# Adding the expert rows in DRAM with an accumulating scatter, instead of storing two rows per token and summing them on TensorE

## The chip, the cores and the metric

The kernel runs on one core of one Trainium2 chip. The metric is the device time of one execution in microseconds (us). Before the change the median of three runs was 1459.46 us (1457.72 to 1459.51).

## The reference

One encoder layer is applied to two sequences, 512 and 1024 tokens of 1024 numbers (T = 1536 tokens in all, 12 tiles of 128). What matters for the change is its last part, the mixture of experts and the norm behind it. Every token chooses one group and in it two of the 32 experts; the outputs of the two are weighted and added.

```python
def block_fn(args):
    tok, w, e = args
    xb = h_pad[tok]
    gu = xb @ w_gate_up[e]
    y = (jax.nn.silu(gu[:, :D_EXPERT]) * gu[:, D_EXPERT:]) @ w_down[e]
    return y * w[:, None]
yb = lax.map(block_fn, (buf_tok..., buf_w..., block_e))
out = jnp.zeros((t_tok + 1, d), h.dtype).at[buf_tok].add(yb.reshape(rows, d))
...
x = layer_norm(ALPHA * x + g2 * moe(h), ln2_g, ln2_b)
```

## The kernel before, in words

There is no scheduler: every engine has its own instruction stream, written out by hand, and the engines meet at semaphores. The stages follow each other.

**Adaptation and input projection.** w_ada comes in 24 pieces of 1 MB (`load_ada`). The first 12 are used ahead of everything else. The other 12 are spread over the first six token tiles of the input projection (`ADA_TILES` = 6, the loop at L427 of the SP queue): each piece goes through one SBUF slot, is split by ScalarE (`ada_h`, L693) and VectorE (`ada_l`, L944), and is multiplied on TensorE (`ada_mm`, L1342 and L1343). The token tiles themselves come through one buffer, `xs` (`load_x`, L399). All these loads leave by one queue, SP's, and each waits until its buffer is free.

**Mixing, second norm, routing.** These write h2 (the experts' input) and x1 (the residual) to DRAM and make a table of the blocks: which 128 token rows each block gathers, where it scatters them, with which weights, and which expert it belongs to. There are 39 blocks here for 32 experts. An unused row of a block has an index that is out of bounds, and its row is not written.

**Expert blocks.** For block i, POOL gathers the rows (`gather`, L645), TensorE transposes them and computes gate and up, then down for block i-1; each product is three matmuls of 512 columns (L1320, L1321, L1322), since the numbers are held as a high and a low part. ScalarE splits the weights (L815, L819), VectorE takes the remainders (L1220, L1224). SP loads 6 MB of weights for each new expert, each piece as soon as its slot is free (L487, L495). ScalarE weighs the result into the one buffer `y_sb` (`weigh`, L846), and POOL scatters it into DRAM (`scatter`, L656). `scatter(i)` waits for the landing of the scatter before it, then copies its indices `s_idx` (L651) and its weights `s_w` (L652), on which `weigh` waits, and then issues the transfer. A pair (token, choice) has a row of its own: `y_rows` has 3072 rows, choice 0 in the first 1536, choice 1 behind them.

**Final stage.** The SP queue loads the second norm's vectors and all 12 tiles of x1 into `fin` (L541) while the last blocks run, waits for all scatters, and loads for each token tile the two rows of each token (`y0`, L547, and `y1`, L548; four slots). TensorE adds them: two products with the identity for each half of 512 columns, four matmuls for a tile, into two banks (L1619, L1620). VectorE multiplies the banks with the gate (`gated`, L1280, 128x512 twice), adds the residual (L1284), and does the norm in a pipeline over the tiles: variance of tile t-1 (L1290), gain of tile t-1 (L1294), scale and shift of tile t-2 (L1299). ScalarE squares (L895) and stores the tiles, POOL takes the power -0.5 (L675).

## Time and profile before

| | |
|---|---|
| median of three runs | 1459.46 us (1457.72 to 1459.51) |
| time of the profiled execution | 1457.56 us |
| its span | 1455.8 us |
| mean granted TensorE clock | 0.94 |
| TensorE matmul | 1266.5 us busy, 87% of the span |
| TensorE weight load | 1030.7 us, 71% |
| VectorE | 932.9 us, 64% |
| ScalarE | 653.3 us, 45% |
| GpSimd (POOL) | 280.3 us, 19% |
| read from and written to DRAM | 297.47 MB and 39.37 MB |

The first 657 us hold projection, mixing and routing, the stretch from 657 to 1370 us the expert blocks, and the last 85 us the final stage. A share is an average over these stages, so what bounds each stage is read from a stretch of it. "SPq" is an instruction on the SP queue that issues a transfer; "[4.88 <-DMA ada_raw]" at the end of a timeline row says that the engine stood idle for 4.88 us before it and what ended that.

### The profile page before, as it was taken

To read this page: it belongs to the slowest core of one execution; us is meant where nothing else is said; L and a number is where in the kernel's file an instruction comes from. 1 tells how busy PE (TensorE), PEld (TensorE's weight loads), DVE (VectorE), ACT (ScalarE), POOL (GpSimd) and SP (SyncE) were. 2 spreads that over 40 slices of the span, in tenths; PEclk is the share of its full clock that TensorE was granted. 3 is DMA by queue.
4 is the path that set the end of the run, shared out by engine and by line. 5 is a ranking of instruction groups with operands and counts; after the bars stand their busy time and mean duration, and the time that the engine had idled before them with its cause. 6 is when DMAs were issued, how large, how long until landed. Compare 5 with 4: busy or idle time off the path is not lost.

```text
span 1455.8 us, 22916 instructions
## 1 busy us (share of the span) xinstructions
PE 1266.5 (87%) x6239; PEld 1030.7 (71%) x6240; DVE 932.9 (64%) x1025; ACT 653.3 (45%) x635; POOL 280.3 (19%) x321
## 2 busy tenths in 40 slices
PE   4479999999789799426999999999999999999592
PEld 3367888788668588325888888888888888888440
DVE  7655544443356455595657875765478888888188
ACT  5532322111212112215556765665478888887222
POOL 6100000000024344241111211111112111222122
PEclk9889999999989899558999999999999999999896
DMA  9642231000233432634769996877689999998793
GB/s 296 246 143 93 96 102 57 18 29 1 92 125 116 144 115 101 243 132 168 263 245 344 402 366 226 307 261 269 226 342 396 398 397 395 388 406 310 307 348 138
DMA packets 111712, 329.44 MB, mean 226 GB/s; under 512 B 12192, under 2 KB 37952, under 8 KB 111680
## 3 DMA queue, kind: packets, MB, share of 16 engines
q1 hardware_dynamic: 98288, 288.63, 53.4%
q0 software_dynamic: 11520, 34.09, 6.3%
q10 hardware_dynamic: 1872, 6.29, 1.1%
q8 instruction: 20, 0.33, 0.1%
q14 instruction: 12, 0.10, 0.0%
HBM read 297.47 MB, written 39.37 MB: 231 GB/s over the span
## 4 chain that ended last, share of the span: by engine, by line
PE 77%; DVE 14%; DMA 3%; issue 2%; ACT 2%; POOL 1%; SPq 1%; DVEq 0%; POOLq 0%; ACTq 0%
PE bank L1320 21%; PE bank L1322 21%; PE bank L1321 21%; PE bank L1552 2%; PE bank L1342 1%; PE bank L1343 1%; PE bank L1516 1%; PE bank L1574 1%; DVE ada_l L944 1%; DVE hT L968 1%; DVE fin L1284 1%; DVE fin L1299 1%; DVE gated L1280 1%; PE bank L1407 1%; ACT ada_h L693 1%
## 5 line engine op out<-in xcount | busy, mean ns | idle before, releaser
L1220 DVE TENSOR_TENSOR gu_l<-gu_raw,gu_h x124 | 278.5, 2287 | 39.7 <-ACT gu_h L815 39.7
L1320 PE MATMUL bank<-gu_h,xT_h 128*128 (+1 forms) x624 | 248.1, 398 | 4.1 <-DVE xT_l L1239 4.1
L1322 PE MATMUL bank<-gu_h,xT_l 128*128 (+1 forms) x624 | 244.5, 392 | 0.0
L1321 PE MATMUL bank<-gu_l,xT_h 128*128 (+1 forms) x624 | 243.9, 391 | 0.0
L815 ACT ACTIVATE gu_h<-gu_raw (+1 forms) x128 | 238.4, 1924 | 5.2 <-issue 5.2
L1224 DVE TENSOR_TENSOR dn_l<-dn_raw,dn_h (+1 forms) x64 | 143.6, 2285 | 5.9 <-ACT dn_h L819 5.9
L1320 PEld LDWEIGHTS bank<-gu_h,xT_h 128*128 128x128 f32 x624 | 117.8, 189 | 28.1 <-DVE xT_l L1239 2.9
L1320 PE MATMUL bank<-win_h,hT_h 128*128 128x512 f32 x288 | 117.4, 408 | 22.5 <-DMA pool_s<-in_pool_scale 22.5
L1322 PEld LDWEIGHTS bank<-gu_h,xT_l 128*128 128x128 f32 x624 | 117.7, 189 | 25.5
L1321 PEld LDWEIGHTS bank<-gu_l,xT_h 128*128 128x128 f32 x624 | 118.0, 189 | 23.7
L819 ACT ACTIVATE dn_h<-dn_raw (+1 forms) x64 | 119.0, 1914 | 33.9 <-DVE table_i L1215 33.8
L1320 PE MATMUL bank<-dn_h,aT_h 128*128 (+1 forms) x312 | 125.6, 402 | 2.5 <-DVE aT_l L1234 2.5
L1322 PE MATMUL bank<-dn_h,aT_l 128*128 (+1 forms) x312 | 122.5, 393 | 0.0
L1321 PE MATMUL bank<-dn_l,aT_h 128*128 (+1 forms) x312 | 122.4, 392 | 0.0
L1322 PE MATMUL bank<-win_h,hT_l 128*128 128x512 f32 x288 | 114.4, 397 | 0.0
L1321 PE MATMUL bank<-win_l,hT_h 128*128 128x512 f32 x288 | 114.4, 397 | 0.0
L656 POOL DMA_INDIRECT y_rows<-y_sb,s_idx x39 | 66.7, 1710 | 221.1 <-ACT y_sb L846 221.1
L825 ACT ACTIVATE act_s<-bank 128x512 f32<-128x512 f32 x39 | 23.3, 597 | 183.4 <-PE bank L1322 183.4
L1320 PE MATMUL bank<-wout_h,z_h 128*128 128x512 f32 x192 | 79.1, 412 | 14.3 <-DVE z_l L1063 14.3
L944 DVE TENSOR_TENSOR ada_l<-ada_raw,ada_h 128x2048 fp32r<-128x2048 f32 x24 | 55.2, 2307 | 45.0 <-ACT ada_h L693 44.8
L1230 DVE TENSOR_TENSOR act_a<-bank,act_s 128x512 f32<-128x512 f32 x39 | 27.0, 691 | 85.7 <-ACT act_s L825 85.7
L1320 PEld LDWEIGHTS bank<-win_h,hT_h 128*128 128x128 f32 x288 | 55.1, 191 | 34.3 <-DMA pool_s<-in_pool_scale 22.8
(226 smaller groups left out, 2144.5 us busy)
## 6 DMA issues: line engine op xcount, KB each, us to landing
gu_raw<-in_w_gate_up SPq DMA_DIRECT2D x128, 1024.0 KB, 7.5
dn_raw<-in_w_down SPq DMA_DIRECT2D x64, 1024.0 KB, 7.5
ada_raw<-in_w_ada SPq DMA_DIRECT2D x24, 1024.0 KB, 5.5
y<-y_rows SPq DMA_DIRECT2D x24, 512.0 KB, 5.4
win_raw<-in_w_in SPq DMA_DIRECT2D x8, 768.0 KB, 6.9
h_rows<-h SPq DMA_DIRECT2D x12, 512.0 KB, 2.7
x_rows<-x SPq DMA_DIRECT2D x12, 512.0 KB, 3.6
fin<-x_rows SPq DMA_DIRECT2D x12, 512.0 KB, 13.7
```

What stands on the lines that cost most here:

```text
L656: nc.gpsimd.indirect_dma_start(out=y_d, out_offset=bass.IndirectOffsetOnAxis(ap=s_idx[:, 0:1], axis=0), in_=y_sb[:], in_offset=None, bound ...
L815: nc.scalar.activation(gu_slot(gu_h, e, c), gu_slot(gu_raw, e, c), ACT.Copy).then_inc(S["gu_split_h"], 1)
L819: nc.scalar.activation(dn_slot(dn_h, e, c), dn_slot(dn_raw, e, c), ACT.Copy).then_inc(S["dn_split_h"], 1)
L825: nc.scalar.activation(act_s[:], ps[0][:], ACT.Silu).then_inc(S["silu_made"], 1)
L944: nv.tensor_tensor(ada_l[slot][:], ada_raw[slot][:], ada_h[slot][:].bitcast(F32), ALU.subtract).then_inc(S["ada_split_l"], 1)
L1220: nv.tensor_tensor(gu_slot(gu_l, e, c), gu_slot(gu_raw, e, c), gu_slot(gu_h, e, c).bitcast(F32), ALU.subtract).then_inc(S["gu_split_l"], 1)
L1224: nv.tensor_tensor(dn_slot(dn_l, e, c), dn_slot(dn_raw, e, c), dn_slot(dn_h, e, c).bitcast(F32), ALU.subtract).then_inc(S["dn_split_l"], 1)
L1230: nv.tensor_tensor(act_a[:], ps[1][:], act_s[:], ALU.mult).then_inc(S["act_ready"], 1)
L1320: mm(out, lh, rh, start=start, stop=False)
L1321: mm(out, lh, rl, start=False, stop=False)
L1322: return mm(out, ll, rh, start=False, stop=stop)
L1552: last = nc.tensor.transpose(ps[2 + k // 4][:, (k % 4) * P:(k % 4 + 1) * P], xg[:, k * P:(k + 1) * P], ident[:])
```

## The change

1. `y_rows` has 1536 rows, one per token, and both choices of a token have the same row index (the iota at L620 has step 0 between them in place of T).
2. The indirect transfer of `scatter` gets `compute_op=ALU.add`: it adds the block's rows to what is in DRAM. Blocks stay apart, since each waits for the one before it to land, and one block holds a token once.
3. The rows must be zero first. POOL clears a tile `zeros` (128x128) at its very start, and SP writes it into `y_rows` with 12 transfers of 512 KB, two in front of each turn of the `ADA_TILES` loop. Each transfer reads the 512 B of a partition eight times. POOL waits for them before the first gather.
4. The final stage loads one tile of rows per token tile in place of two, TensorE has no part in it, and VectorE multiplies `y0` in SBUF with the gate in one instruction of 128x1024. The slot of `y0` is free once `gated` is made.

```diff
-        TOP0 = top // 32 * 32 - 3744
+        TOP0 = top // 32 * 32 - 3744 - 4 * ZN
...
-        y_d = nc.dram_tensor("y_rows", (PAIRS, D), F32).ap()
+        y_d = nc.dram_tensor("y_rows", (T, D), F32).ap()
...
             load_ada(N_ADA1)
             load_x(1, 0)
+            sp.wait_ge(S["zeros_made"], 1)
             for t in range(ADA_TILES):
+                for n in range(t * NT // ADA_TILES, (t + 1) * NT // ADA_TILES):
+                    sp.dma_start(y_d[n * P:(n + 1) * P, :].rearrange("p (c n) -> p c n", n=ZN), zeros[:, None, :].to_broadcast([P, D // ZN, ZN])).then_inc(S["y_zeroed"], 16)
                 load_x(t + 2, 0 if t + 2 < SEQ_TILES[0][1] else 1)
                 load_ada(N_ADA1 + 2 * t + 1)
...
                 if t >= F_SLOTS:
-                    sp.wait_ge(S["y_summed"], t - F_SLOTS + 1)
+                    sp.wait_ge(S["f_gated"], t - F_SLOTS + 1)
                 sp.dma_start(y0[s][:], y_d[bass.ds(t * P, P), :]).then_inc(y_loaded[s], 16)
-                sp.dma_start(y1[s][:], y_d[bass.ds(T + t * P, P), :]).then_inc(y_loaded[s], 16)
...
+            pool.memset(zeros[:], 0.0).then_inc(S["zeros_made"], 1)
             st.done(pool.memset(ident[:], 0.0))
...
-            nc.gpsimd.iota(tok[:], pattern=[[T, 2], [P, NT]], base=0, channel_multiplier=1,
+            nc.gpsimd.iota(tok[:], pattern=[[0, 2], [P, NT]], base=0, channel_multiplier=1,
...
-                                             in_=y_sb[:], in_offset=None, bounds_check=PAIRS - 1,
-                                             oob_is_err=False).then_inc(S["y_scattered"], 16)
-
+                                             in_=y_sb[:], in_offset=None, bounds_check=T - 1,
+                                             oob_is_err=False, compute_op=ALU.add).then_inc(S["y_scattered"], 16)
+
+            pool.wait_ge(S["y_zeroed"], 16 * NT)
             gather(0, first=True)
...
-                dve.wait_ge(S["y_summed"], t + 1)
-                for b in range(2):
-                    c = slice(512 * b, 512 * (b + 1))
-                    last = nv.tensor_tensor(gated[:, c], ps[bank + b][:], g2b[q][:, c], ALU.mult)
+                dve.wait_ge(y_loaded[t % F_SLOTS], 16 * (t // F_SLOTS + 1))
+                if t >= 1:
+                    dve.wait_ge(S["f_taken"], t)
+                last = nv.tensor_tensor(gated[:], y0[t % F_SLOTS][:], g2b[q][:], ALU.mult)
                 last.then_inc(S["f_gated"], 1)
...
-            for t in range(NT):
-                slot, bank = t % F_SLOTS, 2 * (t % F_BANKS)
-                pe.wait_ge(y_loaded[slot], 32 * (t // F_SLOTS + 1))
-                if t >= F_BANKS:
-                    pe.wait_ge(S["f_gated"], t - F_BANKS + 1)
-                for b in range(2):
-                    n = slice(512 * b, 512 * (b + 1))
-                    mm(ps[bank + b][:], ident[:], y0[slot][:, n], start=True, stop=False)
-                    last = mm(ps[bank + b][:], ident[:], y1[slot][:, n], start=False, stop=True)
-                last.then_inc(S["y_summed"], 1)
```

The SP queue at the start of the `ADA_TILES` loop (`ada_raw` is a piece of w_ada, `xs` a token tile), before:

```order
L399 DMA xs<-in_x_prompt 128x1024 [waits xT_made] x2
L394 DMA ada_raw_69<-in_w_ada 128x8x256 [waits ada_used] x2
L399 DMA xs<-in_x_prompt 128x1024 [waits xT_made]
L394 DMA ada_raw_69<-in_w_ada 128x8x256 [waits ada_used] x2
L399 DMA xs<-in_x_sample 128x1024 [waits xT_made]
```

and after:

```order
L400 DMA xs<-in_x_prompt 128x1024 [waits xT_made]
L432 DMA y_rows<-zeros 1024x1x128 [waits zeros_made]
L432 DMA y_rows<-zeros 1024x1x128
L400 DMA xs<-in_x_prompt 128x1024 [waits xT_made]
L395 DMA ada_raw_69<-in_w_ada 128x8x256 [waits ada_used] x2
L432 DMA y_rows<-zeros 1024x1x128 x2
L400 DMA xs<-in_x_prompt 128x1024 [waits xT_made]
L395 DMA ada_raw_69<-in_w_ada 128x8x256 [waits ada_used] x2
L432 DMA y_rows<-zeros 1024x1x128 x2
L400 DMA xs<-in_x_sample 128x1024 [waits xT_made]
```

In the first turn the two writes stand behind a token tile; in the other five they stand right behind the second of two pieces of w_ada and ahead of the next token tile.

VectorE at the start of the final stage, before:

```order
L1280 TENSOR_TENSOR gated<-bank,g2b_218 128x512 [waits y_summed,last_loaded]
L1280 TENSOR_TENSOR gated<-bank,g2b_218 128x512
L1284 SCALAR_TENSOR_TENSOR fin_204,f_sum<-fin_204,gated 128x1024 [waits x1_loaded0,f_gated]
L1286 TENSOR_SCALAR f_mean<-f_sum 128x1 [waits f_taken]
L1280 TENSOR_TENSOR gated<-bank,g2b_218 128x512 [waits y_summed]
```

and after:

```order
L1285 TENSOR_TENSOR gated<-y_0_197,g2b_215 128x1024 [waits y_loaded0,last_loaded]
L1289 SCALAR_TENSOR_TENSOR fin_201,f_sum<-fin_201,gated 128x1024 [waits x1_loaded0,f_gated]
L1291 TENSOR_SCALAR f_mean<-f_sum 128x1 [waits f_taken]
L1285 TENSOR_TENSOR gated<-y_1_198,g2b_215 128x1024 [waits f_taken,y_loaded1]
L1289 SCALAR_TENSOR_TENSOR fin_202,f_sum<-fin_202,gated 128x1024 [waits x1_loaded0,f_gated]
```

Two instructions on banks have become one on a loaded tile, and what it waits for is the load itself.

## Rows read from the trace of the kernel before

**Rows 1.** The page's chain that ended last: shares of the span.
```profile
PE 77%; DVE 14%; DMA 3%; issue 2%; ACT 2%; POOL 1%; SPq 1%; DVEq 0%; POOLq 0%; ACTq 0%
```
**Rows 2.** Timeline from last block to second tile: start us, us, engine, line, operation, [idle].
```profile
1368.32 0.18 POOL L651 COPY s_idx<-table_i 128x1 int32 x1 [6.50 <-DMA y_rows<-y_sb,s_idx]
1368.44 0.18 POOL L652 COPY s_w<-table 128x1 f32 x1
1368.98 1.26 ACT L846 ACTIVATE y_sb<-bank,s_w 128x512 f32<-128x512 f32 x2 [8.58 <-PE bank L1322]
1371.13 0.99 POOL L656 DMA_INDIRECT y_rows<-y_sb,s_idx  x1 [2.51 <-ACT y_sb L846]
1378.36 0.33 SPq L547 DMA_DIRECT2D y<-y_rows  x1
...
1383.27 2.07 PE L1619 MATMUL bank<-y,ident 128*128 128x512 f32 x2 [14.40 <-DMA y<-y_rows]
...
1388.85 1.29 DVE L1280 TENSOR_TENSOR gated<-bank,g2b 128x512 f32<-128x512 f32 x2 [27.40 <-PE bank L1620]
...
1390.17 1.23 DVE L1284 SCALAR_TENSOR_TENSOR fin<-fin,gated 128x1024 f32<-128x1024 f32 x1
...
1392.21 1.29 DVE L1280 TENSOR_TENSOR gated<-bank,g2b 128x512 f32<-128x512 f32 x2 [0.62 <-PE bank L1620]
```
**Rows 3.** Groups of VectorE by form: xcount, busy us, mean ns of one, idle before.
```profile
L1280 DVE TENSOR_TENSOR gated<-bank,g2b 128x512 f32<-128x512 f32 x24 | 15.4, 683 | 28.0 <-PE bank L1620 28.0
...
L962 DVE TENSOR_TENSOR hT_l<-hT,hT_h 128x1024 fp32r<-128x1024 f32 x12 | 14.6, 1218 | 0.0
```
**Rows 4.** Windows, us: PE, PEld, DVE, ACT, POOL busy, clock, DMA share, GB/s.
```profile
1062.56:1328.36 265.80, 265.80 (x1261) 220.97 (x1261) 237.82 (x151) 211.87 (x181) 54.49 (x75) 1.00 1.01 394
1368.00:1377.00 9.00, 0.86 (x4) 0.38 (x2) 0.00 (x0) 1.26 (x2) 1.30 (x3) 0.79 1.03 413
```
**Rows 5.** DMA view, 1060 to 1350 us: queue's packets, MB; issues, us to landing.
```profile
q0 software_dynamic: 4752, 12.55, 11.3%
...
gu_raw<-in_w_gate_up SPq DMA_DIRECT2D x61, 1024.0 KB, 7.6
...
y_rows<-y_sb,s_idx POOLq DMA_INDIRECT x17, 8.3
```
**Rows 6.** DMA view, 1360 to 1379 us, two scatters: POOL's queue.
```profile
q0 software_dynamic: 396, 1.02, 13.5%
```
**Rows 7.** Timeline of one expert block, 1148 to 1168 us.
```profile
1149.00 2.15 POOL L656 DMA_INDIRECT y_rows<-y_sb,s_idx  x1 [6.05 <-ACT y_sb L846]
1149.69 8.55 SPq L487 DMA_DIRECT2D gu_raw<-in_w_gate_up  x4
...
1159.15 1.91 ACT L815 ACTIVATE gu_h<-gu_raw  x1
...
1164.56 1.27 ACT L846 ACTIVATE y_sb<-bank,s_w 128x512 f32<-128x512 f32 x2
```
**Rows 8.** Timeline, 2 to 9 us: a transfer with later ones queued behind it.
```profile
2.40 0.58 SPq L402 DMA_DIRECT2D w_spT<-in_w_spatial  x1
3.02 8.25 SPq L394 DMA_DIRECT2D ada_raw<-in_w_ada  x4
...
8.07 1.12 PE L1332 MATMUL bank<-ident,w_spT 128*128 128x128 f32 x4 [4.32 <-DMA w_spT<-in_w_spatial]
```
**Rows 9.** Timeline of one piece of w_ada, and the window while it moves.
```profile
103.85 0.38 SPq L394 DMA_DIRECT2D ada_raw<-in_w_ada  x1
...
109.12 1.91 ACT L693 ACTIVATE ada_h<-ada_raw 128x2048 fp32r<-128x2048 f32 x1 [4.88 <-DMA ada_raw<-in_w_ada]
```
```profile
106.00:107.00 1.00, 1.00 (x6) 0.83 (x5) 0.00 (x0) 0.00 (x0) 0.00 (x0) 1.00 1.06 371
```
**Rows 10.** Timeline, 0 to 2 us: POOL's clear and VectorE's first work.
```profile
0.77 0.20 POOL L553 MEMSET ident<- 128x128 f32 x1 [0.29 <-POOLq L1635]
...
1.79 0.23 DVE L921 TENSOR_SCALAR bands<-band_prev 128x128 f32<-128x128 f32 x1 [1.67 <-POOL band_prev L559]
```

More of the change, by code:

```diff
@@ L53 @@
 F_SLOTS = 4
+ZN = 128
 F_BANKS = 4
@@ L170, in encoder @@
         half_neg = r.take("half_neg", [P, 1])
+        zeros = r.take("zeros", [P, ZN])
         r = Region(C1)
@@ L288, in encoder @@
         y0 = [r.take(f"y0_{s}", [P, D]) for s in range(F_SLOTS)]
-        y1 = [r.take(f"y1_{s}", [P, D]) for s in range(F_SLOTS)]
         fin = [r.take(f"fin{t}", [P, D]) for t in range(NT)]
@@ L329, in encoder @@
         S = {n: sem(n) for n in (
-            "c_loaded small_loaded ada_bias c_silu cT_made biasT_made cT_high cT_low bias_copied pair_sum_made ada_split_h ada_split_l mod_hl_made mod_cols mod_made modT_made ident_made"
+            "zeros_made y_zeroed c_loaded small_loaded ada_bias c_silu cT_made biasT_made cT_high cT_low bias_copied pair_sum_made ada_split_h ada_split_l mod_hl_made mod_cols mod_made modT_made ident_made"
             " consts_made mod_row mod_stored wsp_loaded wspT_made wspT_copied band_edge"
@@ L348, in encoder @@
             " y_idx y_scattered"
-            " last_loaded y_summed f_gated f_taken f_centre f_squared f_var f_rstd_made f_gained f_ready f_stored"
+            " last_loaded f_gated f_taken f_centre f_squared f_var f_rstd_made f_gained f_ready f_stored"
             " dve_steps pool_steps dve_carrier pool_carrier sp_carrier"
@@ L1275, in f_residual @@
             def f_residual(t):
-                q, bank = 0 if t < SEQ_TILES[0][1] else 1, 2 * (t % F_BANKS)
-                dve.wait_ge(S["y_summed"], t + 1)
-                for b in range(2):
-                    c = slice(512 * b, 512 * (b + 1))
-                    last = nv.tensor_tensor(gated[:, c], ps[bank + b][:], g2b[q][:, c], ALU.mult)
+                q = 0 if t < SEQ_TILES[0][1] else 1
+                dve.wait_ge(y_loaded[t % F_SLOTS], 16 * (t // F_SLOTS + 1))
+                if t >= 1:
+                    dve.wait_ge(S["f_taken"], t)
+                last = nv.tensor_tensor(gated[:], y0[t % F_SLOTS][:], g2b[q][:], ALU.mult)
                 last.then_inc(S["f_gated"], 1)
```

## The prediction

> **What bounds the kernel now.** I began with the chain that ended last [rows 1]: TensorE carries 77% of the span and VectorE 14%, so removing TensorE work pays only where TensorE is the last to finish. The matmuls that go are in the final stage, so I read its timeline [rows 2]. The last scatter is issued at 1371.13, the first load of y leaves at 1378.36 when it has landed, TensorE begins at 1383.27 and VectorE at 1388.85. From there VectorE sets the end: of the 28.0 us that it stands idle ahead of its 24 instructions on `gated` [rows 3], 27.40 are ahead of tile 0 and 0.62 ahead of tile 1, so later tiles wait for nothing. So the sum is on the path only at the stage's start. Then the windows of the expert blocks [rows 4]: from 1062.56 to 1328.36, which I chose as 15 blocks of 17.72 us with a new expert each, TensorE is busy for all of it, and the DMA engines show a share of 1.01 at 394 GB/s. That is the second thing to see. TensorE bounds the blocks, but the transfers are nearly full as well, and the change alters a transfer there. Last, the early loads [rows 8, 9], beside which the zeros are written.
>
> **The final stage.** In 1378.36 to 1388.85 there are two parts. TensorE's first sum takes 1388.85 - 1383.27 = 5.58 us and goes. The load before it takes 4.91 us for two transfers of 0.52 MB; with one to wait for, 0.52 MB less at the 413 GB/s of a full queue [rows 4] is 1.27 us less, 3.64 us. So VectorE starts 10.49 - 3.64 = **6.85 us** earlier after the scatter's landing. This holds if transfers of one queue finish in the order of issue; rows 8 bear that out (below). Tile 1 needs the second load, 4.91 us after 1378.36, and VectorE is done with tile 0 at 3.64 + 2.7: its wait of **0.62 us** goes and no other takes its place. The instruction on `gated` changes: the two halves on banks took 1390.17 - 1388.85 = 1.32 us to the start of the next, and the nearest row of one 128x1024 instruction with both inputs in SBUF is `hT_l` with 1.218 us [rows 3], with the 0.03 us to the next 1.25. That is 0.07 us x 12 tiles = **0.8 us**; if it takes as long as the pair it is 0. The added wait on `f_taken` costs nothing, since the instruction ahead of it in VectorE's own queue has waited for the same count. Loads of tiles 4 to 11 now wait for `gated` of three tiles before, some 14 us ahead of their use (three tiles of four instructions of about 1.2 us) against a landing of 4 to 5 us. Together -8.3 us.
>
> **The scatter.** No row shows an accumulating transfer. I call x what it takes longer to land than a plain one. It is paid twice at the end. `s_idx` of the last block waits for the scatter before it until 1368.32, `s_w` is done at 1368.62, and `weigh` starts at 1368.98 because of TensorE: 0.36 us of cover, then every microsecond is on the path. The last scatter pays x again before the loads of y. So 2x - 0.36 us. The bound below is x = 0: the same bytes are written. For the value: an addition in DRAM must read the 0.51 MB that it writes. The two last scatters moved 1.02 MB [rows 6], and the queue is full with the x1 tiles until 1377, at 413 GB/s; 0.51 MB more is 1.24 us. I take x = 1.3. The bound above is that the transfer takes as long again as the whole landing, 7.2 us (1371.13 to 1378.36). I stay near the lower end because most of the 7.2 us is not bytes of the scatter (0.51 MB is 1.24 us of it) but issue, the other queue's packets and completion, which an addition does not repeat. **+2.2 us**.
>
> The Trainium skill ("Collectives: The Full Stack", the bandwidth ceiling) has a rule that speaks against this change: the adding unit itself costs nothing, but the addition needs two source reads on the same read ring, which halved the measured rate of a reduction against a copy (1.93 times). By it each scatter's data phase doubles, which is near the x I took; no row here shows it.
>
> **The scatters inside the expert blocks.** Latency is covered: a scatter issued at 1149.00 lands 8.3 us later [rows 5] and the next writing of `y_sb` is at 1164.56, 15.56 us later [rows 7]; an x up to 7 us is free. Throughput is the question. From 1060 to 1350 POOL's queue moved 12.55 MB, of which 16 gathers of 128 rows are 8.39, so a scatter carries 0.245 MB there, 60 rows. Reading them once more is 0.60 us of the DMA engines per block. A block moves 394 GB/s x 17.72 us = 6.98 MB, which at 413 GB/s takes 16.90 us; to spare are 0.82 us (I round the uncertainty of both rates down to **0.7 us**). It just fits, so **0**. If the cover is gone, each block is longer by what exceeds 0.7 us, less once the slack of the tightest load: the fourth piece of gate and up is issued at 1149.69 and wanted at 1159.15, 9.46 us, against a landing of 7.6, so 1.9 us.
>
> **The zeros.** POOL's clear of 128x128 takes 0.20 us [rows 10] and stands ahead of the constants with which VectorE's chain starts at 1.79: **+0.2 us**, which may be absorbed later. The 12 writes: two each right behind a piece of w_ada, five times. That piece is on the path at least once (issued 103.85; ScalarE had stood idle for 4.88 us when it landed at 109.12) [rows 9]. If a queue serves its transfers in order, the zeros behind it cost nothing; the token tile behind them has over 20 us until its use. Rows 8 speak for order: w_spT landed at 8.07, 5.67 us after its issue, though 4 MB were queued behind it from 3.02 on, which alone would take over 11 us at 371 GB/s. I take **0**. The bound above: the zeros share the engines evenly with the piece, 1.05 MB more at 371 GB/s, 2.8 us x 5 = 14 us. Below zero there is nothing, since nothing is taken away.
>
> **What else is moved.** SP issues 12 transfers more early and 12 fewer at the end; no one waits for that queue's issue time in either place. POOL's wait for the zeros is met hundreds of microseconds before its first gather. 48 matmuls fewer leave TensorE idle at a time when nobody wants it.
>
> **The sum.** -8.3 + 2.2 + 0 + 0.2 + 0 = **-5.9 us**. The profiled execution took 1457.56 us (span 1455.8 and 1.8 around it), which gives 1451.7. The median of the runs shown lies 1.9 above it; against that I expect **1453.6 us**. A difference of about 0.2% (2.9 us) is what a measurement of this kernel can tell from none.
>
> **The rivals.**
>
> *Slow addition, felt at the end only.* x is 3.5 to 5 us, say because read, add and write of a row follow one another. The path from scatter to scatter is short and exposed, for this; the small share of bytes in the landing speaks against. -8.1 + 2x - 0.36 gives -1.5 to +1.5, around the median, 1459.5. Break-even is at x = 4.2. Chance 0.16.
>
> *The expert blocks become bound by DMA (slower).* For it: share 1.01 and only 0.7 us to spare where the read alone takes 0.6. Against it: the rate reaches 413 where the queue is certainly full, and most blocks have landings well ahead of use. If an addition occupies the engines for 1.5 us more per 60 rows (2.5 times one read), 15 blocks x 0.8 = 12 less 1.9 is +10.1; in the tail x is then 3.1 (twice the rows): -8.1 + 5.8 = -2.3. Together +7.8, 1467 us. It turns to slower than before above 1.1 us per scatter, where blocks cost 4.1 and x is 2.3. Chance 0.19.
>
> *The zeros delay w_ada.* All five pieces share the engines: +14 on -5.9 is +8, 1467.6; a third of it eats the gain to -1.2. For it: the two engines' reads and writes could run side by side, and the packets are 512 B. Against it: rows 8. Chance 0.10.
>
> *The addition costs nothing at all* (x below 0.5): -8.1, 1451.4. It is part of my forecast's lower end.
>
> **How the numbers follow.** Forecast 0.55, between -8.5 and -3: 1451 to 1456.5. The slow addition gives 0.13 of "same" and 0.03 of "slower"; of the zeros' 0.10 I put 0.03 in "same" and 0.07 in "slower"; the blocks' 0.19 is slower. Faster by over 0.2% 0.56, within 0.15, slower 0.29. The range goes from 1450 (the whole gain, and the 1.4 us by which single runs differ) to 1467 (the middle of the two slower cases), which leaves out about 0.05 below and 0.15 above.
>
> **What would show it.** Right: no L1619 on TensorE, `gated` starting some 3.6 us after the first load of y, one instruction of about 1.22 us per tile in place of the pair, `s_idx` of the last block some 1.3 us after the old interval from its scatter's issue (7.5 us), the windows of 17.72 us unchanged with TensorE busy throughout and 410 GB/s, ScalarE's wait for w_ada still 4.9 us. Wrong: idle time on TensorE in the expert blocks, or ScalarE and VectorE waiting for gu_raw; a median landing of the scatter above 12 us; ScalarE waiting more than 6 us for a piece of w_ada.

## The result, and the profile after

| | before | after |
|---|---|---|
| median | 1459.51 us (1457.72 to 1460.86, 9 runs) | 1463.5 us (1461.84 to 1467.5, 9 runs) |
| ratio | | 1.0031, 95% interval 1.002 to 1.0041 |
| profiled execution, span | 1457.56, 1455.8 us | 1467.5, 1465.7 us |

The change makes the kernel slower by 4.0 us, where 5.9 us less was forecast. The profiled execution lies 4 us above its median, so lengths of single stretches are read from it, and totals from the medians. Lines of the changed kernel stand about five higher (three matmuls L1325 to L1327, `gu_h` L820, `y_sb` L851, the scatter L660, `gated` L1285).

First the page of the changed kernel: busy time by engine, and the chain that ended last.

```profile
PE 1230.0 (84%) x6143; PEld 1014.9 (69%) x6144; DVE 929.1 (63%) x1013; ACT 653.7 (45%) x635; POOL 322.7 (22%) x322
...
PE 75%; DVE 14%; DMA 4%; issue 3%; ACT 2%; SPq 1%; POOL 1%; DVEq 0%; POOLq 0%; ACTq 0%
...
q0 software_dynamic: 11520, 34.10, 9.2%
```

Beside [rows 1], DMA and issue each have 1% more of the chain and TensorE 2% less. TensorE's busy time fell by 36.5 us, and the kernel is slower all the same. POOL's queue q0, in the third row, took 6.3% of the engines' span before.

The final stage, in the timeline from the last two blocks to the first tile (start us, us, engine, line, operation, idle before), answers to [rows 2]:

```profile
1375.66 1.91 POOL L660 DMA_INDIRECT y_rows<-y_sb,s_idx  x1 [4.65 <-ACT y_sb L851]
...
1385.44 0.18 POOL L655 COPY s_idx<-table_i 128x1 int32 x1 [7.87 <-DMA y_rows<-y_sb,s_idx]
1385.56 0.18 POOL L656 COPY s_w<-table 128x1 f32 x1
1385.91 1.26 ACT L851 ACTIVATE y_sb<-bank,s_w 128x512 f32<-128x512 f32 x2 [10.66 <-POOL s_w L656]
1389.03 1.61 POOL L660 DMA_INDIRECT y_rows<-y_sb,s_idx  x1 [3.29 <-issue]
1398.12 7.93 SPq L551 DMA_DIRECT2D y<-y_rows  x6
1401.88 1.22 DVE L1285 TENSOR_TENSOR gated<-y,g2b 128x1024 f32<-128x1024 f32 x1 [25.19 <-DMA y<-y_rows]
```

The load of y takes 3.76 us to the first `gated` (10.49 before; 3.64 forecast), and one instruction of 1.22 us stands for the pair. Ahead of that the stage has grown: 9.78 us from the issue of a scatter to the next `s_idx` (7.51 before), 3.12 us from the start of `y_sb` to the last scatter's issue (2.15 before), and 9.09 us from there to its landing (7.23 before).

The groups by form show that every later tile is as forecast, beside [rows 3]: no idle time but the first tile's.

```profile
L1285 DVE TENSOR_TENSOR gated<-y,g2b 128x1024 f32<-128x1024 f32 x12 | 14.6, 1219 | 25.2 <-DMA y<-y_rows 25.2
```

Now the expert blocks. Windows of the changed kernel (length; PE, PEld, DVE, ACT and POOL busy; clock, DMA share, GB/s), beside [rows 4]:

```profile
1068.68:1130.77 62.09, 62.09 (x297) 51.64 (x297) 55.05 (x35) 46.93 (x41) 13.45 (x17) 1.00 1.02 382
1130.77:1205.52 74.75, 74.75 (x356) 62.12 (x355) 63.58 (x42) 57.01 (x49) 20.52 (x23) 1.00 1.02 392
1205.52:1355.55 150.03, 143.44 (x675) 118.11 (x673) 125.55 (x80) 112.53 (x96) 52.47 (x40) 1.00 0.97 364
```

TensorE is busy throughout in the first two and idle for 6.59 us in the third. Why it comes late is seen in ScalarE's splits of a piece of gate and up (the row that answers to `gu_h` in [rows 7]), block after block:

```profile
1130.77 1.92 ACT L820 ACTIVATE gu_h<-gu_raw  x1 [0.61 <-DMA gu_raw<-in_w_gate_up]
...
1149.79 1.92 ACT L820 ACTIVATE gu_h<-gu_raw  x1 [1.91 <-DMA gu_raw<-in_w_gate_up]
...
1166.94 1.92 ACT L820 ACTIVATE gu_h<-gu_raw  x1 [1.34 <-DMA gu_raw<-in_w_gate_up]
...
1186.50 1.92 ACT L820 ACTIVATE gu_h<-gu_raw  x1 [3.18 <-DMA gu_raw<-in_w_gate_up]
...
1205.52 1.92 ACT L820 ACTIVATE gu_h<-gu_raw  x1 [4.48 <-DMA gu_raw<-in_w_gate_up]
...
1224.54 1.91 ACT L820 ACTIVATE gu_h<-gu_raw  x1 [5.00 <-DMA gu_raw<-in_w_gate_up]
...
1355.55 1.92 ACT L820 ACTIVATE gu_h<-gu_raw  x1 [4.77 <-DMA gu_raw<-in_w_gate_up]
```

In all but one of the steps shown up to 1224.54 the piece lands later than in the block before, until the slack is used up and TensorE waits. The twelve blocks from 1130.77 to 1355.55 follow each other at 18.73 us in the mean, 1.0 us more than the 17.72 of before.

These windows do not hold the whole stage. What it lost is read from the first scatter's issue to the start of `y_sb` of the last block but one, before and then after:

```profile
706.02:1358.65 652.63, 652.63 (x3096) 542.59 (x3095) 486.87 (x325) 442.04 (x395) 119.38 (x185) 1.00 0.85 326
```
```profile
712.37:1373.50 661.13, 654.23 (x3096) 542.80 (x3095) 484.01 (x324) 442.39 (x396) 164.19 (x185) 1.00 0.89 321
```

The same 3096 matmuls take 8.5 us longer: TensorE is idle for 6.9 us and its matmuls are busy for 1.6 us more.

The view of waits sums it up (us in total, times, longest); its first two rows have no counterpart before, and the third was 32.0, 6, 7.8:

```profile
ACT gu_h L820 <- DMA gu_raw<-in_w_gate_up: 52.5, 16, 5.2
...
PE bank L1325 <- issue: 6.9, 6, 1.3
...
ACT ada_h L698 <- DMA ada_raw<-in_w_ada: 37.6, 6, 8.7
```

That third row is the early stage. A piece of w_ada with zeros behind it, beside [rows 9]:

```profile
107.25 0.38 SPq L395 DMA_DIRECT2D ada_raw<-in_w_ada  x1
...
107.67 2.48 SPq L432 DMA_DIRECT2D y_rows<-zeros  x2
113.30 1.91 ACT L698 ACTIVATE ada_h<-ada_raw 128x2048 fp32r<-128x2048 f32 x1 [5.67 <-DMA ada_raw<-in_w_ada]
```

6.05 us from the piece's issue to its use, where it was 5.27. So time was lost in three places: the blocks, the two scatters at the end, and w_ada. Each was costed at little or nothing. The experiments ask how much each is worth, and by what mechanism.

### The profile page after: what moved, and what is told of

Read it like the earlier page. It is cut to its first block, busy times and chain, and to the rows that moved or that the text cites. A ratio compares the mean times of both kernels' runs of the same rounds, so it can differ in the third digit from the quotient of the medians.

```text
span 1465.7 us, 22716 instructions
## 1 busy us (share of the span) xinstructions
PE 1230.0 (84%) x6143; PEld 1014.9 (69%) x6144; DVE 929.1 (63%) x1013; ACT 653.7 (45%) x635; POOL 322.7 (22%) x322
## 3 DMA queue, kind: packets, MB, share of 16 engines
HBM read 291.18 MB, written 45.66 MB: 230 GB/s over the span
## 4 chain that ended last, share of the span: by engine, by line
PE 75%; DVE 14%; DMA 4%; issue 3%; ACT 2%; SPq 1%; POOL 1%; DVEq 0%; POOLq 0%; ACTq 0%
PE bank L1325 21%; PE bank L1327 21%; PE bank L1326 21%; PE bank L1557 2%; DMA ada_raw<-in_w_ada 2%; DVE ada_l L949 2%; PE bank L1347 2%; PE bank L1521 1%; PE bank L1348 1%; DMA y_rows<-y_sb,s_idx 1%; ACT ada_h L698 1%; PE bank L1579 1%; DVE fin L1289 1%; DVE hT L973 1%; DVE gated L1285 1%
## 5 line engine op out<-in xcount | busy, mean ns | idle before, releaser
L820 ACT ACTIVATE gu_h<-gu_raw (+1 forms) x128 | 238.1, 1917 | 57.7 <-DMA gu_raw<-in_w_gate_up 52.5
L1325 PE MATMUL bank<-gu_h,xT_h 128*128 (+1 forms) x624 | 248.1, 398 | 11.0 <-issue 6.9
L1327 PE MATMUL bank<-gu_h,xT_l 128*128 (+1 forms) x624 | 244.5, 392 | 0.0
L660 POOL DMA_INDIRECT y_rows<-y_sb,s_idx x39 | 90.6, 2324 | 248.3 <-ACT y_sb L851 245.0
L1325 PEld LDWEIGHTS bank<-gu_h,xT_h 128*128 128x128 f32 x624 | 117.8, 189 | 36.5 <-issue 10.1
L1325 PE MATMUL bank<-win_h,hT_h 128*128 128x512 f32 x288 | 117.8, 409 | 22.2 <-DMA pool_s<-in_pool_scale 22.2
L1327 PEld LDWEIGHTS bank<-gu_h,xT_l 128*128 128x128 f32 x624 | 117.7, 189 | 25.4
L1325 PE MATMUL bank<-dn_h,aT_h 128*128 (+1 forms) x312 | 125.4, 402 | 2.9 <-DVE aT_l L1239 2.9
L1327 PE MATMUL bank<-dn_h,aT_l 128*128 (+1 forms) x312 | 122.5, 393 | 0.0
L1327 PE MATMUL bank<-win_h,hT_l 128*128 128x512 f32 x288 | 114.8, 399 | 0.0
L1325 PE MATMUL bank<-wout_h,z_h 128*128 128x512 f32 x192 | 79.2, 412 | 14.3 <-DVE z_l L1068 14.3
L949 DVE TENSOR_TENSOR ada_l<-ada_raw,ada_h 128x2048 fp32r<-128x2048 f32 x24 | 55.1, 2298 | 53.7 <-ACT ada_h L698 53.7
L646 POOL COPY g_idx<-table_i 128x1 int32 (+1 forms) x41 | 19.8, 482 | 275.2 <-PE bank L1557 252.9
L580 POOL TENSOR_TENSOR v_rstd<-v_mv,half_neg 128x1 f32<-128x1 f32 x12 | 6.6, 548 | 332.3 <-DVE v_mv L1016 332.3
```

What stands on the lines that cost most here:

```text
L660: nc.gpsimd.indirect_dma_start(out=y_d, out_offset=bass.IndirectOffsetOnAxis(ap=s_idx[:, 0:1], axis=0), in_=y_sb[:], in_offset=None, bound ...
L820: nc.scalar.activation(gu_slot(gu_h, e, c), gu_slot(gu_raw, e, c), ACT.Copy).then_inc(S["gu_split_h"], 1)
L949: nv.tensor_tensor(ada_l[slot][:], ada_raw[slot][:], ada_h[slot][:].bitcast(F32), ALU.subtract).then_inc(S["ada_split_l"], 1)
L1325: mm(out, lh, rh, start=start, stop=False)
L1327: return mm(out, ll, rh, start=False, stop=stop)
```

## The experiments

The runs stand beside executions of the kernel before of their own, so they are compared by their ratios; "against before" is the ratio less one, times 1459.5 us. "From the first scatter on" is the profile's span less the issue of the first scatter, which leaves out the early stage. That stage differs by chance: the first scatter is issued between 705.70 and 709.17 us in the kernels without early zeros. The last column is of one execution each; those of "addition alone" and "two scatters" lie 3.2 and 3.5 us above their medians, and that of "the change, again" 2.9, so the ratios say more of these three.

| run | median us | ratio to before, 95% | against before, us | from the first scatter on |
|---|---|---|---|---|
| before, again | 1459.74 | 0.9997 (0.9986 to 1.0007) | -0.4 | 749.95 |
| the change, again | 1464.22 | 1.0028 (1.0017 to 1.004) | +4.1 | 752.9 |
| zeros late | 1462.52 | 1.0021 (1.0012 to 1.003) | +3.1 | 752.6 |
| plain scatter | 1454.37 | 0.9952 (0.9936 to 0.9969) | -7.0 | 742.0 |
| addition alone | 1470.85 | 1.0075 (1.0062 to 1.0088) | +10.9 | 763.95 |
| two scatters | 1471.28 | 1.0073 (1.0055 to 1.0091) | +10.7 | 764.1 |
| zeros late, x1 late | 1459.65 | 1.0 (0.9991 to 1.0008) | +0.0 | 749.7 |
| early zeros alone | 1463.01 | 1.002 (1.0011 to 1.0029) | +2.9 | 749.9 |
| zeros late, half a gather | 1453.46 | 0.996 (0.9948 to 0.9973) | -5.8 | 745.8 |
| before with x1 late | 1455.93 | 0.9971 (0.9962 to 0.9981) | -4.2 | 746.0 |
| ... and two sums on VectorE | 1454.34 | 0.996 (0.9947 to 0.9974) | -5.8 | 744.8 |
| ... and three sums on VectorE | 1454.44 | 0.9961 (0.9948 to 0.9974) | -5.7 | 744.2 |

### Before and after once more

The two kernels as they are.

> The kernel before once more, for a second profile: how much of the 6 us between the two first profiles at the first scatter (706.0 against 712.4 us) is chance of the early loads. The zeros written late gave 708.5 and 707.7 there. If the early stage varies by itself, this one stands at 706 to 709 us; all behind the first scatter (749.8 us from its issue to the end) should repeat within 1 us. Time as before, 1460 us.

> The changed kernel once more, for a second profile. The first profile (span 1465.7 us, above the median of its runs) had three late places: w_ada pieces (6.2 us behind by the end of the input projection, 3.0 of it before the first write of zeros), the expert blocks (about 7 us of idle time on TensorE, pieces of gate and up landing late) and the two last scatters (2.3 and 2.8 us longer each, with what POOL takes to issue them). Theory A (the accumulating scatter fills the DMA engines in the expert blocks): the idle time in the blocks and the longer scatters are there again within 2 us. Theory B (the writes of zeros beside w_ada): the 3 us behind the first zeros are there again. What came before the first zeros should be gone or smaller if it is chance. Time 1463.5 within 2 us.

Both repeated. The waits for gu_raw in the changed kernel are again 53.7 us in 16 places, and the stretch from the first scatter to `y_sb` of the last block but one is again 8.6 us longer, so they belong to the kernel and not to one execution.

### The zeros written late

```diff
-            sp.wait_ge(S["zeros_made"], 1)
             for t in range(ADA_TILES):
-                for n in range(t * NT // ADA_TILES, (t + 1) * NT // ADA_TILES):
-                    sp.dma_start(y_d[n * P:(n + 1) * P, :]..., zeros...)
...
             with sp.Fori(ADA_TILES + 2, NT) as t:
                 load_x(t, 1)
+            sp.wait_ge(S["zeros_made"], 1)
+            for n in range(NT):
+                sp.dma_start(y_d[n * P:(n + 1) * P, :]..., zeros...)
```

> The 12 writes of zeros stand together in the idle stretch of the SP queue behind the last token tile of the input projection, ahead of w_out; all else as changed. Theory A: only what the zeros cost beside w_ada goes, 1 to 3 us, so 1460.5 to 1462.5, with the expert blocks and the last scatters as late as before. Theory B (the zeros are most of the loss): 6 us less, about 1457.5.

1.0 us less than the change measured beside it, by ratios whose intervals overlap: not to be told from nothing. In the profile the five waits for w_ada are back at 4.8 us and the blocks are nearly as bad as ever: 51.3 us of waiting for gu_raw, and 7.6 us lost up to `y_sb` of the last block but one. So most of the loss lies in the blocks and the tail. This is the kernel on which the next tests build, since it has no early zeros.

### A plain scatter

```diff
-                                             oob_is_err=False, compute_op=ALU.add).then_inc(S["y_scattered"], 16)
+                                             oob_is_err=False).then_inc(S["y_scattered"], 16)
```

The second choice's row then takes the place of the first's: one of the two is missing from each token's sum, and nothing else differs in work.

> The changed kernel with a plain scatter in place of the accumulating one (computation changed: a token keeps only the row of the choice scattered last). Theory A: the expert blocks are back at 17.72 us each with TensorE busy throughout, the last scatters land in 7.2 to 7.5 us, and the final stage's gain of 8.3 us is left, less what the zeros cost: 1452 to 1454.5 us. Theory B: about 1463 us, as changed.

The addition itself is worth 4.1 + 7.0 = 11.1 us. From the first scatter on it is 10.9 us against the change (752.9), 10.6 against the late zeros. The windows from 1070 to 1340, first of this kernel, then with late zeros and the addition:

```profile
1070.00:1340.00 270.00, 270.00 (x1280) 224.47 (x1279) 242.01 (x153) 213.31 (x181) 54.47 (x75) 1.00 1.01 393
```
```profile
1070.00:1340.00 270.00, 265.04 (x1252) 219.32 (x1251) 229.19 (x147) 207.74 (x178) 79.89 (x75) 1.00 1.02 387
```

And their DMA views of the same stretch (queue: packets, MB, share; issues: count, KB, median us to landing), the plain one first:

```profile
q0 software_dynamic: 4320, 11.17, 10.8%
gu_raw<-in_w_gate_up SPq DMA_DIRECT2D x60, 1024.0 KB, 7.4
...
y_rows<-y_sb,s_idx POOLq DMA_INDIRECT x15, 8.5
```
```profile
q0 software_dynamic: 4176, 11.01, 14.3%
gu_raw<-in_w_gate_up SPq DMA_DIRECT2D x58, 1024.0 KB, 13.0
y_rows<-y_sb,s_idx POOLq DMA_INDIRECT x15, 10.3
```

About the same megabytes and packets, but 3.5% more of 270 us of all 16 engines: 9.45 us over 15 scatters, **0.63 us** for one of 60 rows. This is the low end: over the whole execution q0 has 9.2% of the engines' 1465.7 us in the changed kernel and 6.3% of 1454.1 us here, 43 us more over 39 scatters of 79 rows in the mean, or about 0.84 us for 60 rows. That the addition takes engine time, and that gate and up land 5.6 us later with it, is shown. What the cause was could still be two things: engine time, or the later landing of the scatter itself (10.3 for 8.5).

In the final stage, this kernel's timeline gives what the change would do with a scatter like the old one:

```profile
1366.85 1.00 POOL L660 DMA_INDIRECT y_rows<-y_sb,s_idx  x1 [5.23 <-ACT y_sb L851]
1374.75 0.18 POOL L655 COPY s_idx<-table_i 128x1 int32 x1 [6.90 <-DMA y_rows<-y_sb,s_idx]
1374.87 0.18 POOL L656 COPY s_w<-table 128x1 f32 x1
1375.22 1.26 ACT L851 ACTIVATE y_sb<-bank,s_w 128x512 f32<-128x512 f32 x2 [8.78 <-POOL s_w L656]
1377.37 0.99 POOL L660 DMA_INDIRECT y_rows<-y_sb,s_idx  x1 [2.32 <-ACT y_sb L851]
1384.77 5.42 SPq L551 DMA_DIRECT2D y<-y_rows  x5
1388.62 1.22 DVE L1285 TENSOR_TENSOR gated<-y,g2b 128x1024 f32<-128x1024 f32 x1 [21.14 <-DMA y<-y_rows]
```

The intervals from issue to landing are 7.90 and 7.40, near the 7.51 and 7.23 of before the change, and the load takes 3.85. Up to `y_sb` of the last block but one this kernel takes 652.63 us, to the hundredth what the kernel before takes: the blocks' loss is the addition's.

### The addition alone, in the kernel before

```diff
-                                             oob_is_err=False).then_inc(S["y_scattered"], 16)
+                                             oob_is_err=False, compute_op=ALU.add).then_inc(S["y_scattered"], 16)
```

All 3072 rows are zeroed late, with 24 writes; the final stage stays as before.

> The kernel before with the accumulating scatter alone: two rows per token as before, summed on TensorE, 3072 rows zeroed in the idle stretch ahead of w_out. Theory A: slower than before by the idle time in the expert blocks and twice the longer scatter, 7 + 4.6 = about 11 us, 1468 to 1472 us. Theory B: 1460 us, as before. In between: the share of the accumulating scatter, free of the final stage's gain.

It costs 10.9 us beside the old final stage, as between the change and its plain twin (11.1). The 24 late writes are in it too; by the agreement they cost little.

### Two plain scatters per block

```diff
+        y2_d = nc.dram_tensor("y2_rows", (PAIRS, D), F32).ap()
...
                                              oob_is_err=False).then_inc(S["y_scattered"], 16)
+                nc.gpsimd.indirect_dma_start(out=y2_d, out_offset=bass.IndirectOffsetOnAxis(ap=s_idx[:, 0:1], axis=0),
+                                             in_=y_sb[:], in_offset=None, bounds_check=PAIRS - 1,
+                                             oob_is_err=False).then_inc(S["y_scattered"], 16)
```

The kernel before writes the same rows a second time to a tensor that nothing reads (the waits for the scatters count both): the engines get more to do without any addition.

> The kernel before with a second plain scatter of the same rows into another tensor, issued right behind the first. It moves as many bytes more per block as the addition reads (0.245 MB, 0.6 us of the engines), without any addition. Theory A1 (the engines were full and had less than 0.6 us to spare in a block): ScalarE waits for gate and up pieces and TensorE is idle some 5 to 7 us in the expert blocks, as with the addition; time 1467 to 1473 us with the tail. Theory A2 (it is the addition itself, its latency or its dependent read, that holds the queues up): blocks stay at 17.72 us, and only the tail is longer, 1461 to 1465 us.

```profile
1070.00:1340.00 270.00, 263.48 (x1244) 217.86 (x1243) 227.02 (x146) 204.98 (x175) 109.02 (x88) 1.00 1.01 397
```
```profile
ACT gu_h L820 <- DMA gu_raw<-in_w_gate_up: 58.2, 17, 5.2
```

Its window and its waits are those of the addition, at 14.1% of engine time on q0. The scatters land in 8.6 us here, as plain ones do. So more engine time on POOL's queue is enough to break the blocks, whether it adds or not. Note the rate as well: 397 GB/s over this window with the engines full, not 413.

### Half a gather, beside the addition

```diff
-        h2_d = nc.dram_tensor("h2_rows", (T, D), F32).ap()
+        h2_d = nc.dram_tensor("h2_rows", (T, D // 2), F32).ap()
...
-                sp.dma_start(h2_d[bass.ds(t * P, P), :], h2[:]).then_inc(S["h2_stored"], 16)
+                sp.dma_start(h2_d[bass.ds(t * P, P), :], h2[:, 0:512]).then_inc(S["h2_stored"], 16)
...
-                nc.gpsimd.indirect_dma_start(out=xg[:], out_offset=None, in_=h2_d,
+                nc.gpsimd.indirect_dma_start(out=xg[:, 0:512], out_offset=None, in_=h2_d,
...
+            st.done(pool.memset(xg[:, 512:1024], 0.0))
```

> The changed kernel with its zeros written late, and the second norm stores and each block gathers only the first 512 of the 1024 columns of a token's row; the other 512 columns of xg are set to zero once, so that the experts work on half of each row. A block then moves 0.25 MB less, about what an addition costs the DMA engines more. Theory A (the blocks lose time because the addition takes engine time that was not to be had): the waits for gu_raw (51 us in the run with late zeros) fall under 10 us, TensorE is busy all of 1070 to 1340, and the time falls by 5 to 8 us against that run: ratio to before 0.996 to 0.999 where it was 1.0021 (a part of it from the shorter stores in the second norm). Rival B (the blocks lose time because a scatter that adds lands later, and y_sb, s_w or the gather behind it come late, or because additions hold the queue up in another way than by their time): waits for gu_raw stay above 35 us, ratio 1.001 to 1.002.

```profile
1070.00:1340.00 270.00, 270.00 (x1280) 224.44 (x1279) 237.75 (x152) 213.60 (x181) 72.36 (x76) 1.00 1.00 372
```
```profile
q0 software_dynamic: 3360, 7.24, 11.0%
...
y_rows<-y_sb,s_idx POOLq DMA_INDIRECT x15, 10.3
```

This is the test in the other direction. The addition is still there and lands as late as with full gathers (10.3 us), but q0's share is back at 11.0% and TensorE is busy for all 270 us; of the 7.6 us that the blocks lost with late zeros 0.9 are left. From the first scatter on it takes 745.8 us against 752.6, which is 6.8 less, inside the 5 to 8 expected; the rest of the 8.9 us between their ratios belongs to the early stage (shorter stores of h2, and chance), which was not taken apart. The expected drop of the waits for gu_raw under 10 us did not come: 27.7 us are left, but no longer enough to reach TensorE. The later landing of the scatter is thereby ruled out as the cause in the blocks.

### The early zeros alone

The kernel before, with the `zeros` tile and the early writes as the change has them:

```diff
+            sp.wait_ge(S["zeros_made"], 1)
             for t in range(ADA_TILES):
+                for n in range(t * NT // ADA_TILES, (t + 1) * NT // ADA_TILES):
+                    sp.dma_start(y_d[n * P:(n + 1) * P, :]..., zeros...)
```

> The kernel before plus the early zeros alone: the 12 writes of 512 KB stand where the change puts them, the scatter stays plain and the final stage as before. Theory C (each pair behind a piece of w_ada delays that piece's landing by some 0.8 us, five times, and ScalarE and TensorE have no slack there): 2 to 4 us slower than before, ratio 1.0015 to 1.003, the waits for ada_raw 36 to 38 us instead of 32. Rival D (the 4 us in the profiles of the early stage are the spread among executions, and the queue serves in order as predicted): ratio 1.000 within 0.001.

2.9 us slower, 1.6 to 4.2 by the interval. ScalarE's wait in the same place as in [rows 9]:

```profile
105.89 0.38 SPq L396 DMA_DIRECT2D ada_raw<-in_w_ada  x1
106.31 2.41 SPq L433 DMA_DIRECT2D y_rows<-zeros  x2
111.95 1.91 ACT L700 ACTIVATE ada_h<-ada_raw 128x2048 fp32r<-128x2048 f32 x1 [5.68 <-DMA ada_raw<-in_w_ada]
```

The other four such waits are 5.60, 5.62, 5.72 and 5.64 us, where they were 4.8 to 4.9. From the split at 85.43 to that at 234.55 it is 149.12 us, and 147.47 in the kernel before (83.44 to 230.91): +1.65. In the same places of the changed kernel it is 150.06, +2.6. In the four profiled kernels with early zeros the stretch takes 149.12 to 150.06, in the ten others 146.84 to 147.96: 2.2 us between the means. By the two comparisons of totals it is 1.0 to 2.9; I count the zeros with 2.2. The first scatter comes at 711.93 to 712.42 us in those four and at 705.70 to 709.17 in the others, 4.3 us between the means, so half of that difference lies outside this stretch, and no run says what makes it. From the first scatter on the kernel takes 749.9 us, as before. That the zeros delay the piece ahead of them is shown; whether by sharing the engines or DRAM wasn't tried.

### x1 loaded late

Ahead of the last scatters the queue still holds twelve x1 tiles of 0.52 MB. Here only four are loaded ahead, and the others behind loads of y. First in the changed kernel with late zeros (both groups behind the first four y loads), then in the kernel before (behind the fourth and the seventh tile):

```diff
-            for t in range(NT):
-                sp.dma_start(fin[t][:], x1_d[bass.ds(t * P, P), :]).then_inc(x1_loaded[t // 4], 16)
+            def load_x1(g):
+                for t in range(4 * g, 4 * g + 4):
+                    sp.dma_start(fin[t][:], x1_d[bass.ds(t * P, P), :]).then_inc(x1_loaded[t // 4], 16)
+
+            load_x1(0)
...
                 sp.dma_start(y1[s][:], y_d[bass.ds(T + t * P, P), :]).then_inc(y_loaded[s], 16)
+                if t == 3:
+                    load_x1(1)
+                elif t == 6:
+                    load_x1(2)
```

> The change with zeros late (e2) and only the first 4 tiles of x1 loaded ahead of the wait for the scatters, the other 8 behind the first four loads of y. If the last two accumulating scatters land late because they share the engines with the x1 tiles, they land in about 6 us in place of 9 to 10 and 4 to 6 us are saved: 1457 to 1459 us. If an accumulating scatter is slow by itself (its rows one after another), they stay at 9 to 10 us and the time at 1462. The idle time of TensorE in the expert blocks (5.9 us) stays by both.

> The kernel before with 8 of the 12 tiles of x1 loaded behind the first loads of y, nothing else. The last scatter lands in 4 to 5 us in place of 7.2, the one before it is covered but for 0.36 us. 2 to 3 us less than before: 1457 to 1458 us. If x1 tiles do not hold the scatter up, 1460.

Both gained: 3.1 us with the addition (from +3.1 to 0.0 against before), 4.2 us without. That is less than the 4 to 6 expected with the addition and more than the 2 to 3 expected without it. From the first scatter on it is 2.9 and 4.0. With the addition, issue, landing and first `gated`:

```profile
1382.64 1.61 POOL L666 DMA_INDIRECT y_rows<-y_sb,s_idx  x1 [3.29 <-issue]
1389.11 1.75 SPq L554 DMA_DIRECT2D y<-y_rows  x4
```

and in the kernel before:

```profile
1373.88 1.00 POOL L663 DMA_INDIRECT y_rows<-y_sb,s_idx  x1 [2.32 <-ACT y_sb L853]
1377.11 0.33 SPq L550 DMA_DIRECT2D y<-y_rows  x1
...
1387.77 1.29 DVE L1287 TENSOR_TENSOR gated<-bank,g2b 128x512 f32<-128x512 f32 x2 [23.64 <-PE bank L1627]
```

A plain scatter that meets an empty queue lands in 3.23 us in place of 7.23, so 4.0 us of the old landing were x1 tiles. One that adds takes 6.47 there. So an addition costs 3.2 us in an empty queue, 1.9 to 2.3 behind a full one (1.7 to 1.9 beside the plain twin). The blocks are untouched by this (55.2 us of waits for gu_raw with the addition), as they must be.

### Sums on VectorE

TensorE's first sum takes 5.58 us in the kernel before (1383.27 to 1388.85). TensorE had stood idle for 14.40 us, and the granted clock was 0.50, the lower of its two levels, from 1381 to 1383 and 0.68 in the mean over the sum. So VectorE makes it itself for the first tiles, in the kernel before with x1 late:

```diff
+                if t < DVE_SUMS:
+                    dve.wait_ge(y_loaded[t], 32)
+                    nv.tensor_tensor(y0[t][:], y0[t][:], y1[t][:], ALU.add).then_inc(S["y_added"], 1)
+                    dve.wait_ge(S["y_added"], t + 1)
+                    last = nv.tensor_tensor(gated[:], y0[t][:], g2b[q][:], ALU.mult)
```

> The kernel before with tiles 4 to 11 of x1 loaded behind the first y loads (as in the run before this one that did only that, ratio 0.9971), and the first two tiles of the final stage summed by VectorE itself (one tensor_tensor of 128x1024 each) and not by TensorE, which is cold there. Theory (the first tile waits 4 x 1.2 us for four matmuls at 1.2 GHz and VectorE then reads the banks): the addition on VectorE costs 1.22 us, gated in SBUF 1.22 us against 2 x 0.68; the first gated comes about 10.66 - 3.7 - 1.2 = 5.8 us after the last scatter lands rather than 10.66, of which the second tile gives 1.2 back: 3 to 4 us less than that run, ratio to before 0.994 to 0.996. Rival (the final stage is set by the rate at which x1 and y arrive, not by the first sum): no gain over that run, ratio 0.997.

> The kernel before with tiles 4 to 11 of x1 loaded behind the first y loads and the first three tiles of the final stage summed by VectorE (two in the run before this one, which left VectorE idle for 3.14 us ahead of the third while TensorE, cold, summed it from 1387.81 to 1394.3). Theory: VectorE's own sum of the third tile costs 1.23 us and is ready at the latest when TensorE would have begun, so 1.9 us of the 3.14 go: 1.5 to 2 us less than with two, ratio 0.9945 to 0.9955 (with two 0.996). Rival: the tiles behind it then wait for their loads, and nothing is gained: ratio 0.996.

The start is what was expected, the gain is not. Timeline with two sums:

```profile
1382.18 1.23 DVE L1289 TENSOR_TENSOR y<-y,y 128x1024 f32<-128x1024 f32 x1 [17.58 <-DMA y<-y_rows]
...
1394.37 1.29 DVE L1296 TENSOR_TENSOR gated<-bank,g2b 128x512 f32<-128x512 f32 x2 [3.14 <-PE bank L1636]
```

VectorE begins 4.96 us after the first load leaves, 5.7 earlier than with TensorE's sum. It pays 2 x 1.23 for the sums and 3.14 for a new wait, since TensorE only begins on the third tile when its rows have landed. That leaves 0.1 us, and 0.7 with the second tile's old wait of 0.62, which is gone; the profile shows 0.8 (76.8 us from the first load to the end, 77.6 without) and the ratios 1.6, in different comparisons. With three sums the new wait is gone, and the third sum's 1.22 us and a wait of 1.30 us for TensorE at the eighth tile take most of its place: 76.3 us in the profile, and no gain that the ratios tell. Both kernels are 0.4% faster than before and 0.7% faster than the change with the whole computation done, and every row stored apart as before: the fastest versions found.

## Why the prediction was wrong, step by step

- **The final stage, -8.3 us: right.** The load takes 3.76 us (3.64), and from the first `gated` to the last it is 51.80 us where it was 53.21, so 1.41 less; 0.62 + 0.8 were forecast. Together 8.1. From the first scatter on, the plain twin takes 7.8 us less than the kernel before. One thing was in no sum: the span ends 3.1 to 3.2 us behind VectorE's last instruction in all seven profiled kernels whose scatter adds or is made twice, and 4.7 to 4.8 us behind it in the seven others, before and plain twin among them. The profiles do not say why; it favours the change by 1.7 us.
- **The scatter at the end, +2.2 us: too small by some 3 us.** x was 2.3 us at the first of the two and 1.9 at the second, not 1.3, and the last issue comes 0.97 us later after `y_sb`. That POOL's part of a scatter gets longer was not in the sum ("issue, the other queue's packets and completion, which an addition does not repeat"). And the cover of 0.36 us between `s_w` and `y_sb` was none. Where `s_w` alone decides, `y_sb` starts 0.35 us after `s_w` does (1374.87 to 1375.22 in the plain twin, 1385.56 to 1385.91 after), and with x1 late it does so too (1371.38 to 1371.73), where the trace names TensorE as the releaser. In [rows 2] the same two rows stand 0.54 apart, so at most 0.2 us of cover were there. Together 2.3 + 1.9 + 1.0 = 5.2, less that; from the issue of the last scatter but one to the landing of the last it is 22.46 us for 17.55, so 4.9.
- **The expert blocks, 0: this is the step that failed, and it turned the sign.** The cost of one scatter was about right: 0.60 us for reading 60 rows again, 0.63 measured in the same window (0.84 over the whole execution). The spare was wrong. "A block moves 6.98 MB, which at 413 GB/s takes 16.90 us; to spare are 0.82 us" took its rate from a window of 9 us with x1 tiles. With weights, gathers and scatters in the mixture, the windows of 265.8 and 270 us without an addition reached 386 to 397 GB/s at a share of 0.99 to 1.01, the one with two plain scatters the most (50 us of blocks with more rows to scatter, 800 to 850 in the kernel before, show 405 at a share of 1.02, so the rate is no constant of the mixture). At 397, the 6.98 MB take 17.58 us, so 0.14 us were to spare; at the 394 of [rows 4] itself nothing was, and the share of 1.01 there said so. The prediction's own rule then gives (0.63 - 0.14) x 15 - 1.9 = 5.5 us, and 7.6 with no spare. Measured are 8.5 us in the changed kernel (8.6 in its second profile, 7.6 and 7.7 in the two with late zeros), of which the window from 1070 to 1340 shows only 270 - 264.2 = 5.8 as idle time. So the mechanism is shown, by the plain twin, the two plain scatters and the half gather, but the rule is too coarse for the size: the blocks follow each other 1.0 us later and not 0.5, and how the loss divides between a scatter dearer than 0.63 us and a smaller spare was not separated. The rival "the expert blocks become bound by DMA" was the case, but its condition (a scatter of 1.1 us or more) was not met: 0.63 to 0.84 was enough.
- **The zeros, 0: wrong by about 2 us.** The pieces of w_ada were on the path, five times, and each came 0.8 us later (under the 2.8 of even sharing). "If a queue serves its transfers in order, the zeros behind it cost nothing": mostly in order is what rows 8 show, not entirely. Five times 0.8 is 4.0 us, and about half of it lengthened the stage.
- **The memset, +0.2 us** is too small to be seen.

The sum with what the profiles show: -8.1 + 4.9 + 8.5 + 2.2 - 1.7 = +5.8, against a measured 4.0 in the medians (by the ratio's interval 2.9 to 6.0). The two agree only within the spread of single executions: the profiled one of the changed kernel lies 4.0 us above its median. For the kernel with late zeros the same sum is -8.3 + 5.3 + 7.6 - 1.7 = +2.9, against 3.1. The marks set for a wrong prediction came up as TensorE's idle time in the blocks and the waits for gu_raw; the landing's median stayed at 10.3, under the mark of 12, and the waits for w_ada at 5.6 to 6.2, around the mark of 6. Those two marks were set too far out, as the terms behind them were.

The Trainium skill ("Collectives: The Full Stack", the bandwidth ceiling) states of the reduction in a collective that its addition needs two source reads on the same read ring, and that it ran at about half the rate of a copy (1.93 times). The transfer here is of another kind, and the runs come near it: 0.245 MB of plain rows are 0.62 us of the engines at 394 GB/s, and the addition takes 0.63 us more in the blocks' window, 0.84 over the whole execution.

## What to carry to other kernels

Before extra bytes are called free beside a busy TensorE, the spare of the transfers must be worked out with the rate that the same stretch reaches when the engines are full; in this kernel a DMA share of 1.01 meant that there was none, though TensorE was busy for all of the window. An overload of 0.5 to 1 us per block is invisible for the first blocks and then costs in nearly each of them, so look at how landings drift, not at one block. And measure a stage from its first event to its last: a window inside it showed 5.8 us of a loss of 8.5. A saving on a path's end may lie in what is queued ahead of its last transfer: moving eight loads gave 4.2 us, with the computation unchanged; what removing TensorE's sum and one load per tile brought (8.1 us) was given back in other stages.

## What the runs showed of the hardware

- A scatter of 60 rows of 4 KB that adds takes 0.63 us more of the 16 DMA engines, with no more packets or bytes in the record (14.3% of the stretch for 4176 packets and 11.01 MB, 10.8% for 4320 and 11.17): each takes longer. Over the whole execution it is 0.84 us for 60 rows.
- It lands 1.8 us later in the blocks (10.3 against 8.5), 3.2 us later on an empty queue (6.47 against 3.23), and GpSimd is longer at it: 1.61 us for 0.99 at the last scatter, and from 1070 to 1340 it is busy for 79.9 us in place of 54.5.
- Writes queued behind a load on the same queue delayed it a little: a piece of 1 MB was used 6.05 us after its issue with 1 MB of zeros behind it, 5.27 without.
- The same 270 us window reads 393 GB/s with plain scatters and 387 with additions, at a share of 1.01 and 1.02, and the pages of the two kernels count the same 291.18 MB read and 45.66 MB written: the bytes counted don't include what an addition reads, so the GB/s alone would have shown a relief where there was an overload.
